# Mixture-of-experts stage of a two-block kernel: half of the tokens through all experts on TensorE with gates from one-hot products, the other half by gathered rows in the same loop

## The reference, cut to what matters

```python
def peer(h, w_q, subkeys, u, v):
    ...
        q = (xc @ w_q).reshape(C, PEER_HEADS, 2, PEER_HALF)
        s = jnp.einsum('chpd,hpnd->chpn', q, subkeys, preferred_element_type=jnp.float32)
        sv, si = lax.top_k(s, PEER_TOPK)
        ...
        g = jax.nn.softmax(best, axis=-1)
        ue = jnp.take(u, ids, axis=0)
        ve = jnp.take(v, ids, axis=0)
        a = jax.nn.gelu(jnp.einsum('cd,chkd->chk', xc, ue), approximate=False)
        return jnp.einsum('chk,chkd->cd', (g * a).astype(xc.dtype), ve)
```

## Time and profile before

| | |
|---|---|
| median of 3 runs | 5263.25 us (5241.67 to 5272.82) |
| the profiled execution | 5242.71 us |
| its span | 5240.9 us |
| busy: PE, DVE, ACT, POOL | 2551.8, 2583.4, 789.0, 1333.2 us |
| moved by DMA | 779.76 MB, of it 536.94 MB by the gathers (queue q0) |
| mean granted TensorE clock | 0.662 |

### The profile page before, as it was taken

The page is one execution under the profiler, slowest core; times in us unless marked ns, Lnnn a source line. Parts: engine busy times, 40 slices in busy tenths (PEclk is TensorE's granted clock), DMA queues, the critical chain, the costliest instruction groups (busy, mean ns, idle before and its releaser), DMA issues. The chain is left out here.

```text
span 5240.9 us, 36566 instructions
## 1 busy us (share of the span) xinstructions
PE 2551.8 (49%) x10726; PEld 1892.2 (36%) x10726; DVE 2583.4 (49%) x4263; ACT 789.0 (15%) x1093; POOL 1333.2 (25%) x1122
## 2 busy tenths in 40 slices
PE   6599359997598259896753896710000000000001
PEld 5367237775366238771541675610000000000000
DVE  2122524322122633321324423388888888788787
ACT  2122113212022113210211322200000000000000
POOL 0010000000010000000000100001877877877875
PEclk9655579998755579998875857855555555555555
DMA  3310012223210013215223101301999999999996
GB/s 103 108 30 5 17 56 96 91 78 109 84 30 17 17 54 97 91 66 210 98 90 86 32 3 40 104 21 64 340 360 350 342 343 345 323 362 357 327 353 254
DMA packets 243145, 779.76 MB, mean 149 GB/s; under 512 B 36915, under 2 KB 49875, under 8 KB 238805
## 3 DMA queue, kind: packets, MB, share of 16 engines
q0 software_dynamic: 147456, 536.94, 28.2%
q1 hardware_dynamic: 91828, 234.68, 13.8%
q10 hardware_dynamic: 3744, 6.69, 0.3%
HBM read 744.38 MB, written 32.24 MB: 148 GB/s over the span
## 5 line engine op out<-in xcount | busy, mean ns | idle before, releaser
L1675 POOL DMA_INDIRECT sbuf<-peer_u,sbuf x512 | 647.9, 1265 | 709.5 <-issue 709.5
L108 PE MATMUL psum<-sbuf 128*128 128x512 f32 (+1 forms) x1744 | 688.6, 395 | 246.1 <-DVE sbuf L264 115.4
L1496 PE MATMUL psum<-sbuf 128*128 128x128 f32 x64 | 14.9, 379 | 1627.9 <-PEq L1645 1560.2
L1702 DVE CUSTOM_DVE_ANT_0 sbuf<-sbuf 128x1024 f32<-128x1024 f32 x512 | 620.6, 1225 | 152.0 <-DMA sbuf<-peer_u,sbuf 134.0
L1724 DVE SCALAR_TENSOR_TENSOR sbuf<-sbuf 128x1024 f32<-128x1024 f32 x512 | 657.5, 1284 | 73.3 <-DMA sbuf<-peer_v,sbuf 20.7
L109 PE MATMUL psum<-sbuf 128*128 128x512 f32 (+1 forms) x1744 | 684.6, 393 | 0.0
L110 PE MATMUL psum<-sbuf 128*128 128x512 f32 (+1 forms) x1744 | 683.4, 392 | 0.0
L932 POOL TENSOR_TENSOR sbuf<-sbuf 64x768 fp32r<-64x768 f32 (+2 forms) x22 | 29.2, 1329 | 2459.7 <-ACT sbuf L893 2459.7
L1675 POOL DMA_INDIRECT sbuf<-peer_v,sbuf x512 | 587.3, 1147 | 158.7 <-issue 158.7
L1496 PEld LDWEIGHTS psum<-sbuf 128*128 128x128 f32 x64 | 10.2, 164 | 1632.7 <-issue 1628.2
L108 PEld LDWEIGHTS psum<-sbuf 128*128 128x128 f32 x1744 | 334.4, 192 | 326.5 <-DVE sbuf L264 118.0
(11 more groups left out here) (250 smaller groups left out, 3589.6 us busy)
## 6 DMA issues: line engine op xcount, KB each, us to landing
sbuf<-w_ffn SPq DMA_DIRECT2D x88, 512.0 KB, 3.4
sbuf<-w_mod SPq DMA_DIRECT2D x12, 2048.0 KB, 8.4
sbuf<-w_fm SPq DMA_DIRECT2D x46, 512.0 KB, 3.7
sbuf<-w_down SPq DMA_DIRECT2D x16, 1408.0 KB, 6.0
sbuf<-w_out SPq DMA_DIRECT2D x24, 512.0 KB, 3.4
sbuf<-cw SPq DMA_DIRECT2D x4, 2048.0 KB, 9.8
sbuf<-wq SPq DMA_DIRECT2D x16, 512.0 KB, 3.6
sbuf<-peer_u,sbuf POOLq DMA_INDIRECT x512, 6.1
```

Source lines behind the costliest of these rows:

```text
L108: nc.tensor.matmul(acc, w_high(k), x_high(k), start=(k == 0), stop=False)
L1675: pool.indirect_dma_start(rows[:, r, :], None, table, bass.IndirectOffsetOnAxis(ap=pick[:, b, r:r + 1], axis=0)).then_inc(gathered[r], 16)
L1702: nc.vector.tensor_tensor_reduce(out=rows[:, r, :], in0=rows[:, r, :], in1=h_cur[:, :], scale=1.0, scalar=0.0, op0=ALU.mult, op1=ALU.add, ...
```

## The change

Half of the tokens, tiles 0 and 1 (GT = 2), keep the gathered rows: 2 tiles x 2 tables x 128 picks = 512 transfers. Tiles 2 and 3 (256 tokens) go through all 16,384 experts. The tables are streamed once in 128 steps of 128 experts, u from a copy `peer_ut` that is transposed in blocks before the launch. In step s, TensorE makes the 128x256 dot products of the experts with the tokens (`up`, 8 products), ScalarE takes the Gelu, VectorE multiplies by the gates, and TensorE adds the product with the step's rows of v to sums for two tiles in four PSUM banks (`down`, 4 products of 512 columns), which last over all steps.

The gates are a matrix of experts by tokens that is zero but for the picks. For one token it is a product over its picks of a one-hot of the second key with a one-hot of the first key times the weight. The first keys are taken in quarters of 32. One group is 8 tokens of one quarter: VectorE makes one operation of 128x1024 and eight of 128x32, TensorE makes 8 products with 32 columns, ScalarE copies the result into `gate`, which holds two quarters. There are 32 groups to a quarter. The first quarter's 32 groups come ahead of the loop; the others run one per step in the first 96 steps. VectorE uses three gathered rows with each of the first 32 groups and 3.25 on average in each step. The additions of gathered rows alternate between two sums. All loops are written out.

`peer_pick` writes the numbers once for tiles 0 and 1, and the two keys as floats for tiles 2 and 3 (`ids`). The first `turn` has 16 transposes. At the end ScalarE copies the four banks into `u_in`, from which the second `turn` reads.

```diff
+GT = 2
...
-                for f in range(2):
-                    did(nc.vector.scalar_tensor_tensor(
...
+                first, rest = slice(0, GT * T), slice(GT * T, ST * T)
+                tiled = lambda x: x.rearrange("p (t k) -> p t k", k=T)
+                did(nc.vector.scalar_tensor_tensor(stream[:, :, cols], tiled(found[:, 0, first]), float(NKEY),
+                                                   tiled(found[:, 1, first]), ALU.mult, ALU.add))
+                for p in range(2):
+                    did(nc.vector.tensor_copy(ids[:, p, :, cols], tiled(found[:, p, rest])))
...
+HELD = 3
+QUARTER = 32
+GROUP = 8
+def peer_experts(nc, C, hT, h_tok, stream, ids, weights, ut, u, v, u_in, y):
+    DENSE = (ST - GT) * P
+    GROUPS = DENSE // GROUP
...
+    QUARTERS = NKEY // QUARTER
+    ROWS = 2 * GT * PICKS
+    EARLY = 3 * GROUPS
+    tok0 = GT * P
+    def dealt(step):
+        if step < 0:
+            return max(0, EARLY * (step + GROUPS + 1) // GROUPS)
+        return EARLY + (ROWS - EARLY) * (step + 1) // NKEY
+    def row(n):
+        return n // (2 * PICKS), n // PICKS % 2, n % PICKS
     with ExitStack() as ctx:
         sem = Sems(nc, ctx)
         sb = lambda shape, dt=F32: ctx.enter_context(sbuf(nc, shape, dt))
+        rows, odd = sb([P, RING, D]), sb([P, D])
+        v_in = sb([P, HELD, D])
+        gate = sb([P, 2, QUARTER, DENSE])
+        hot, part = sb([P, 2, GROUP, NKEY]), sb([P, 2, GROUP, QUARTER])
+        picked = sb([P, 3, DENSE])
+        act_out, w = sb([P, 2, DENSE]), sb([P, 3, DENSE])
+        dots, dots_g, dots_w = sb([P, GT, PICKS]), sb([P, GT, PICKS]), sb([P, GT, PICKS])
+        a_ps = ctx.enter_context(psum(nc, [P, 2, S], F32))
+        g_ps = ctx.enter_context(psum(nc, [P, 2, S], F32))
+        y_ps = ctx.enter_context(psum(nc, [P, 4, S], F32))
...
         block = ctx.enter_context(nc.Block())
+        def wait_row(eng, n):
+            eng.wait_ge(used[n % RING], n // RING + 1)
+        @block.sync
+        def _(sp):
+            for s in range(NKEY):
+                if s >= HELD:
+                    sp.wait_ge(a_made, s - HELD + 1)
+                sp.dma_start(u_in[:, s % HELD, :], ut[s]).then_inc(u_landed[s % HELD], 16)
+                if s >= HELD:
+                    sp.wait_ge(y_made, s - HELD + 1)
+                sp.dma_start(v_in[:, s % HELD, :], v[s * P:(s + 1) * P, :]).then_inc(v_landed[s % HELD], 16)
         @block.gpsimd
         def _(pool):
+            for n in range(ROWS):
+                t, f, j = row(n)
+                if n >= RING:
+                    wait_row(pool, n - RING)
+                pool.indirect_dma_start(rows[:, n % RING, :], None, (u, v)[f],
+                                        bass.IndirectOffsetOnAxis(ap=stream[:, t, j:j + 1], axis=0)
+                                        ).then_inc(gathered[n % RING], 16)
+        @block.tensor
+        def _(pe):
+            for d in range(ST - GT):
+                for x, src in enumerate((ids[:, 0, d, :], ids[:, 1, d, :], weights[:, GT + d, :])):
+                    mm = nc.tensor.transpose(a_ps[:, d, x * P:(x + 1) * P], src, C.ident[:, :])
+                mm.then_inc(turned, 1)
+            def gates(n):
+                pe.wait_ge(hot_made, (GROUP + 1) * (n + 1))
+                if n >= 2:
+                    pe.wait_ge(gates_taken, n - 1)
+                for j in range(GROUP):
+                    mm = nc.tensor.matmul(g_ps[:, n % 2, j * QUARTER:(j + 1) * QUARTER], hot[:, n % 2, j, :],
+                                          part[:, n % 2, j, :], start=True, stop=True)
+                mm.then_inc(gates_made, 1)
+            def up(s):
+                if s < 2:
+                    pe.wait_ge(copied, 2)
+                else:
+                    pe.wait_ge(gelu_done, s - 1)
+                pe.wait_ge(u_landed[s % HELD], 16 * (s // HELD + 1))
+                for k in range(KT):
+                    mm = nc.tensor.matmul(a_ps[:, s % 2, 0:DENSE], u_in[:, s % HELD, k * P:(k + 1) * P], hT[:, k, tok0:S],
+                                          start=(k == 0), stop=(k == KT - 1))
+                mm.then_inc(a_made, 1)
+            def down(s):
+                pe.wait_ge(w_made, s + 1)
+                pe.wait_ge(v_landed[s % HELD], 16 * (s // HELD + 1))
+                for t in range(ST - GT):
+                    for half in range(2):
+                        mm = nc.tensor.matmul(y_ps[:, 2 * t + half, :], w[:, s % 3, t * P:(t + 1) * P],
+                                              v_in[:, s % HELD, half * S:(half + 1) * S], start=(s == 0), stop=(s == NKEY - 1))
+                mm.then_inc(y_made, 1)
+            for n in range(GROUPS):
+                gates(n)
+            for s in range(NKEY):
+                up(s)
+                if s + GROUPS < QUARTERS * GROUPS:
+                    gates(s + GROUPS)
+                if s:
+                    down(s - 1)
+            down(NKEY - 1)
         @block.scalar
         def _(act):
+            for d in range(ST - GT):
+                act.wait_ge(turned, d + 1)
+                nc.scalar.activation(picked[:, :, d * P:(d + 1) * P],
+                                     a_ps[:, d, 0:3 * P].rearrange("p (x k) -> p x k", x=3), ACT.Copy).then_inc(copied, 1)
+            def take(n):
+                q, g = n // GROUPS, n % GROUPS
+                act.wait_ge(gates_made, n + 1)
+                if q >= 2:
+                    act.wait_ge(w_made, QUARTER * (q - 1))
+                nc.scalar.activation(gate[:, q % 2, :, g * GROUP:(g + 1) * GROUP],
+                                     g_ps[:, n % 2, 0:GROUP * QUARTER].rearrange("p (t i) -> p i t", t=GROUP),
+                                     ACT.Copy).then_inc(gates_taken, 1)
+            def gelu_dots(step):
+                for t in range(GT):
+                    last = 2 * PICKS * t + PICKS
+                    if dealt(step - 1) < last <= dealt(step):
+                        for r in range(RING):
+                            wait_row(act, last - 1 - r)
+                        nc.scalar.activation(dots_g[:, t, :], dots[:, t, :], ACT.Gelu).then_inc(dots_gelu, 1)
+            for n in range(GROUPS):
+                take(n)
+                gelu_dots(n - GROUPS)
+            for s in range(NKEY):
+                act.wait_ge(a_made, s + 1)
+                if s >= 2:
+                    act.wait_ge(w_made, s - 1)
+                nc.scalar.activation(act_out[:, s % 2, :], a_ps[:, s % 2, 0:DENSE], ACT.Gelu).then_inc(gelu_done, 1)
+                if s + GROUPS < QUARTERS * GROUPS:
+                    take(s + GROUPS)
+                gelu_dots(s)
+            act.wait_ge(y_made, NKEY)
+            for b in range(4):
+                nc.scalar.activation(u_in[:, b // 2, b % 2 * S:(b % 2 + 1) * S], y_ps[:, b, :], ACT.Copy).then_inc(y_taken, 1)
         @block.vector
         def _(dve):
+            def one_hot(n):
+                q, g = n // GROUPS, n % GROUPS
+                if n >= 2:
+                    dve.wait_ge(gates_made, n - 1)
+                toks = slice(g * GROUP, (g + 1) * GROUP)
+                nc.vector.tensor_tensor(hot[:, n % 2, :, :], C.iota[:, :].unsqueeze(1).to_broadcast([P, GROUP, NKEY]),
+                                        picked[:, 1, toks].unsqueeze(2).to_broadcast([P, GROUP, NKEY]),
+                                        ALU.is_equal).then_inc(hot_made, 1)
+                for j in range(GROUP):
+                    tok = g * GROUP + j
+                    nc.vector.tensor_scalar(part[:, n % 2, j, :], C.iota[:, q * QUARTER:(q + 1) * QUARTER],
+                                            picked[:, 0, tok:tok + 1], picked[:, 2, tok:tok + 1], ALU.is_equal,
+                                            ALU.mult).then_inc(hot_made, 1)
+            def use_row(n):
+                t, f, j = row(n)
+                r = n % RING
+                sums = (y[:, t, :], odd[:, :])[j % 2]
+                if f and j == 0:
+                    dve.wait_ge(dots_gelu, t + 1)
+                    nc.vector.tensor_tensor(dots_w[:, t, :], dots_g[:, t, :], weights[:, t, :], ALU.mult
+                                            ).then_inc(dots_weighed, 1)
+                    dve.wait_ge(dots_weighed, t + 1)
+                    if t:
+                        dve.wait_ge(summed, t)
+                dve.wait_ge(gathered[r], 16 * (n // RING + 1))
+                if f == 0:
+                    nc.vector.tensor_tensor_reduce(out=rows[:, r, :], in0=rows[:, r, :], in1=h_tok[:, t, :], scale=1.0,
+                                                   scalar=0.0, op0=ALU.mult, op1=ALU.add,
+                                                   accum_out=dots[:, t, j:j + 1]).then_inc(used[r], 1)
+                elif j < 2:
+                    nc.vector.tensor_scalar(sums, rows[:, r, :], dots_w[:, t, j:j + 1], None, ALU.mult).then_inc(used[r], 1)
+                else:
+                    wait_row(dve, n - 2)
```

(32 more changed lines are left out.)

102 lines of the change are left out of this document (18 added, 84 removed).

## The result

The changed kernel takes 4943.44 us (median of 4 runs, 4942.33 to 4945.45), the kernel before beside it 5252.46 us (4 runs, 5241.17 to 5272.82). The ratio is 0.9408, 95% interval 0.9373 to 0.9443. The forecast was faster, with 5036 us and a range of 4930 to 5200: the sign and the range held, and the gain of 309 us was larger than the 227 us forecast. The profiled execution took 4943.09 us, its span is 4941.2 us; against the profiled 5242.71 us of before that is 299.6 us less, where the sum had 216.

The account below looks back on a forecast made before the run. DMA gathers at 345 GB/s were taken to bound the 1558.6 us expert stage. Terms 206 + 6 + 8 + 867 + 250 + 8 gave 1345 us, a span of 5025, 5027 profiled and 5036 as median; range 4930 to 5200 us.

Parts of the forecast that it names:

- The 32 groups ahead, 206 us: Gate groups before the loop: VectorE sets the pace at 6.44 us each, with one-hots 2.69 and three rows at 1.25.
- TensorE's step, 8.83 us: Each of the 96 steps with gates: up 3.63, down 3.42 and gates 1.78 us on TensorE, which sets the pace.
- The 0.2 us of waits a step: In the 96 steps with gates, TensorE waits for VectorE queued behind late rows; added to make 9.03 us a step.
- VectorE's chain: From up's end through Gelu, product, gathered rows and one-hot to the next gates: 7.7 us, 8.64 every fourth step.
- After s = 96, DMA at 7.6 to 7.98 us: In the last 32 steps, without gates, DMA passes TensorE's 7.05 us; taken as 7.8 us a step, 250 us.
- Start, end and outside: Stage start 6 us, its end 8 us; outside it, 3.3 us less from transposes and 1.5 us more in peer_pick.
- its 5.2 us: TensorE's time between up(s) and down(s), said to hide ScalarE's 3.4 us even with two table switches a step.
- A (half clock): Rival: TensorE stays at half clock in the loop, 17.0 then 13.7 us a step, span 5970 us; chance 0.11.
- B (the waits take over): Rival: slower small VectorE operations and late rows make steps 10.5, then 8.5 us; span 5215 us; chance 0.20.
- C: Rival, better than forecast: records at 0.213, gates at 0.44, small operations at 0.094 us; 4896 us; chance 0.07.
- D: Rival: gathers and streamed half run one after the other, 1880 us in all, slower; chance 0.01.
- The last landing of the streams: Table loads of 512 KB, issued two steps ahead, land within 16 us behind 8 queued gathered rows, against two steps of 9.

Follow-up runs that it names:

- e5: The changed kernel with no gathered row used ahead of the loop, so 4 rows in each of the 128 steps: 4876.85 us.
- e6: The changed kernel with VectorE's eight small tensor_scalar operations per group made twice, the second set into an unread tile: 5085.2 us.
- e2: The changed kernel with only the gathered rows; streams, gates and products left out, tiles 2 and 3 get zeros: 4380.95 us.
- e3: The changed kernel without one-hots, gate products and their copies, every gate the same constant: 4697.54 us.
- e9: The kernel before with its expert-stage loops written out and constant waits, all 1024 gathers kept: 5164.19 us, ratio 0.9833.
- e4: The changed kernel with each gate product issued twice, 16 instead of 8 a group, same result: 5150.27 us.
- e1: The changed kernel without the 512 gathers, their dots and additions; tiles 0 and 1 get zeros: 4843.91 us.
- e10: The changed kernel with two buffers instead of three for each streamed table: 5021.09 us.
- e7: The changed kernel with 24 rows ahead of the loop, 4 in each of 96 steps, 104 over the last 32: 4866.14 us.

## Why the prediction was right, and where its sizes were off

The forecast of the profiled execution was 5027 us, measured 4943.1, so 84 us are to be explained. Term by term:

- *The 32 groups ahead, 206 us:* 207 us. Right as a sum, by two errors that cancel, which is luck: a row cost 1.14 to 1.20 us instead of 1.25, and the tensor_scalar with two pointers 1.74 / 8 = 0.218 us instead of 0.183, inside its bounds. That VectorE sets this part is shown by e5 (95 us less without its rows) and e6 (50 us more).
- *TensorE's step, 8.83 us:* 3.45 (up, forecast 3.63) + 1.71 (gates, forecast 1.78) + 3.51 to the next up (down, forecast 3.42) = 8.67. The record of 256 columns is 0.216 us; halving the 512-column row, the value I named and did not take, was right to 1.5%. The gate products go at 0.107 us a record (1.71 / 16), as the short products of the earlier trace rows had it, where the loads held them at 0.111.
- *The 0.2 us of waits a step:* not there. This is the step that failed for the 96 steps: with the record it makes 96 x 0.36 = 35 of the 38 us by which they came out shorter (837 against 875 with the half-clock start). VectorE's chain kept its distance: e6 gives it 0.8 us a step of spare or more, at the upper end of the 0.2 to 1.1 of the prediction.
- *After s = 96, DMA at 7.6 to 7.98 us:* wrong. The step is 6.89 us and TensorE's; DMA moved 398 GB/s there where the sum let it have 345 to 363. The faulty step was to read the 345 GB/s at a share of 0.95 as the DMA's limit. e2 had slices of 410, e3 moved 402 GB/s without holding TensorE up, e5 found the limit at 409, and e9 moved the rows of the old stage itself at 368. It cost the forecast 30 us. The Trainium skill, "HBM Reference", section "Specifications (TRN2)", gives some 358 GB/s as a core's share when both cores of a pair stream and about 425 for one core that streams alone; only one core runs here, and the 409 GB/s of e5 agree with the second figure to 4%, while the 345 to 363 of my sum, read from a stage that the DMA did not set alone, happened to lie at the first.
- *Start, end and outside:* 1.5 us instead of 6, 6 instead of 8, and 11 us less outside the stage than forecast, of which some 9 are drift of stages that were not changed.

Together 38 + 30 + 4.5 + 2 + 11 - 1 = 84.5 us.

One reading of the prediction is wrong at no cost: its 5.2 us lie between up(s) and up(s + 1). Between up(s) and down(s) stand up(s + 1) and a second group of gates as well, 10.6 us by its own terms, so ScalarE and VectorE's product had twice the cover that it gave them.

Of the rivals, A (half clock) did not come: 1.00 in both parts of the changed kernel's loop. Its mechanism is near, though: the clock falls for part of a step in e4, with twice the short products (0.98), and in e6, behind waits of 1.5 us (0.96). The rule of the Trainium skill that was weighed there ("TensorE: Matmul & The Clock Gate", section "A second HAM failure mode: psum-queue depth-cycling") says that small idles between groups of matmuls make the clock swing. e6 agrees with it in kind. The changed kernel's loop cycles the same banks without idles and does not swing, and e4 swings without any idle in its records, which the rule does not cover. The attention rows, which the prediction took to agree with it, have no idle and no swing (150.00 of 150 us busy, 0.50 throughout), so they do not bear on it. Why the clock falls in e4 is open.

The half clock stayed in the groups ahead, as forecast. TensorE had 16 short products there and then 2.6 us of rest; e1 and e5 took the rest away, and the clock was still 0.50. B (the waits take over) is a real mechanism that was not reached: e5 shows it with 4 rows a step in the last 32, for 0.8 us a step. C came true in half: records near 0.213, but neither the cheap small operations nor the cheap gate products. D is excluded by the windows above.

The last landing of the streams was forecast as up to 16 us, against two steps of 9; in the changed kernel the median was 8.5 us for peer_ut and 6.5 for peer_v, and e10 shows that the cover of one step is too little for them.

## What to carry to other kernels

When a queue is busy at 0.95, look whether its issuer goes back to back too, before its rate is taken as the limit: here the same DMA engines gave 409 GB/s where the stage had shown 345. Work that is spread over a loop belongs where the engine that carries it has something to spare, not evenly: dealing the rows by part (e7) gave 77 us for a few lines. Price the third buffer before it is taken away: 78 us here. And count a short wait of TensorE at more than its length: in e6 the clock took about as much again.
